# Output projection of a hybrid encoder layer: four row tiles summed in PSUM, two buffers for x, a new tile order

## The reference

```python
u = rms_norm(h, g_norm); z = u @ w_in
o_att = diff_attention(q, k, v, ...)          # per head: rms_norm(o, sub_norm) * (1 - lam_init)
o_lru = rg_lru_branch(xr, ...)                # two directions of a gated linear recurrence
mix = concatenate([o_att * silu(g_att), o_lru * silu(g_lru)], axis=-1)
h = h + mix @ w_out                           # the output projection
e = (p @ w_ple) * sigmoid(h @ w_pg)
h = h + rms_norm(e, g_ple)
```

## Time and profile before

| What | Value |
|---|---|
| median of 3 runs | 1044.59 us (1044.24 to 1045.69) |
| the profiled execution | 1044.89 us |
| its span | 1043.1 us |
| TensorE busy | 994.5 us (95%) |
| VectorE, ScalarE, GpSimd busy | 676.4, 641.4, 502.6 us |
| mean granted TensorE clock | 0.988 |
| DMA | 158.75 MB, 152 GB/s over the span |

### The profile page before, as it was taken

The page is one execution under the profiler, slowest core; times in us unless marked ns, Lnnn a source line. Parts: engine busy times, 40 slices in busy tenths (PEclk is TensorE's granted clock), DMA queues, the critical chain, the costliest instruction groups (busy, mean ns, idle before and its releaser), DMA issues.

```text
span 1043.1 us, 15702 instructions
## 1 busy us (share of the span) xinstructions
PE 994.5 (95%) x5720; PEld 787.3 (75%) x5720; DVE 676.4 (65%) x1115; ACT 641.4 (61%) x1058; POOL 502.6 (48%) x402
## 2 busy tenths in 40 slices
PE   8999999999999999989999999999979869999996
PEld 7867777777788888877777777777867657777775
DVE  5736766683672341699999999999536672444444
ACT  7747576655631222589999999999446542444442
POOL 1162435436665530265767667666422256554451
PEclk9999999999999999999999999999989889999999
DMA  9641544233347339489756764541857861122221
GB/s 345 266 137 36 172 147 118 100 101 124 111 139 219 104 100 262 129 213 256 202 155 168 179 168 134 139 143 62 282 154 226 279 219 51 45 87 91 74 76 74
DMA packets 108636, 158.75 MB, mean 152 GB/s; under 512 B 10504, under 2 KB 69384, under 8 KB 108552
## 3 DMA queue, kind: packets, MB, share of 16 engines
q1 hardware_dynamic: 108416, 157.75, 50.5%
q10 hardware_dynamic: 144, 0.00, 0.0%
HBM read 106.27 MB, written 48.30 MB: 148 GB/s over the span
## 4 chain that ended last, share of the span: by engine, by line
PE 65%; DVE 16%; issue 9%; DMA 4%; ACT 3%; POOL 1%; SPq 0%; DVEq 0%; POOLq 0%; ACTq 0%
DVE E_ L1895 9%; PE b_ps L2183 6%; PE b_ps L2321 6%; PE b_ps L2323 6%; PE b_ps L2322 6%; PE b_ps L2185 6%; PE b_ps L2184 6%; DMA x_rd<-in_x 3%; PE o_ps L2378 3%; PE s_ps L2334 3%; PE w_ps L2295 3%; PE uT_ps L2258 2%; DVE ratio L1904 2%; PE left_ps L2505 2%; PE left_ps L2508 2%
## 5 line engine op out<-in xcount | busy, mean ns | idle before, releaser
L1371 ACT ACTIVATE E_<-E_,nmax 128x1024 f32<-128x1024 f32 (+1 forms) x184 | 186.6, 1018 | 13.2 <-DVE nmax L1895 13.2
L1895 DVE CUSTOM_DVE_ANT_0 E_<-s_ps,bias 128x1024 f32<-128x1024 f32 (+1 forms) x184 | 188.2, 1056 | 10.0 <-PE s_ps L2334 9.8
L1070 POOL TENSOR_TENSOR E_<-E_,ratio 128x576 f32<-128x576 f32 (+3 forms) x92 | 84.7, 920 | 92.5 <-DVE E_ L1911 92.5
L1073 POOL TENSOR_TENSOR E_<-E_ 128x576 f32<-128x576 f32 (+3 forms) x92 | 103.7, 1127 | 7.2
L2185 PE MATMUL b_ps<-u_hi,wA_lo 128*128 128x512 f32 x256 | 99.8, 390 | 0.0
L2334 PE MATMUL s_ps<-KL,QL 128*128 128x512 f32 x256 | 88.6, 430 | 8.1 <-DVE nmax L1895 8.0
L1386 ACT ACTIVATE WT<-w_ps 128x1024 f32<-128x1024 f32 (+1 forms) x96 | 83.5, 870 | 5.9 <-PE w_ps L2295 5.3
L2183 PE MATMUL b_ps<-u_hi,wA_hi 128*128 128x512 f32 x216 | 85.5, 396 | 0.0
L2295 PE MATMUL w_ps<-ident,E_ 128*128 128x128 f32 x624 | 83.5, 273 | 2.1 <-ACT WT L1386 2.0
L2184 PE MATMUL b_ps<-u_lo,wA_hi 128*128 128x512 f32 x216 | 84.1, 389 | 0.0
L2378 PE MATMUL o_ps<-WT,V 128*64 128x128 f32 x1280 | 84.0, 278 | 0.0
(11 more groups left out here) (338 smaller groups left out, 2613.1 us busy)
## 6 DMA issues: line engine op xcount, KB each, us to landing
QL<-qk_t SPq DMA_DIRECT2D x32, 256.0 KB, 7.0
KL<-qk_t SPq DMA_DIRECT2D x32, 256.0 KB, 8.4
bias<-line_d SPq DMA_DIRECT2D x8, 960.0 KB, 11.7
x_sb<-in_x SPq DMA_DIRECT2D x12, 512.0 KB, 9.0
z_ch<-z_stage SPq DMA_DIRECT2D x24, 256.0 KB, 2.8
qk_t<-qh SPq DMA_DIRECT2D x24, 256.0 KB, 2.3
qk_t<-ql SPq DMA_DIRECT2D x24, 256.0 KB, 2.8
mf<-mix_t SPq DMA_DIRECT2D x24, 256.0 KB, 4.1
```

The source lines that it names most:

```text
L1073: gp.tensor_tensor(one, one, two, ALU.add).then_inc(w_gp, 1)
L1371: act.activation(e, e, ACT.Exp, bias=nmax[:, n % 5, c:c + 1], scale=-1.0, accum_out=sums[:, n % 5, c:c + 1]).then_inc(e_done, 1)
L1895: dve.tensor_tensor_reduce(weights_at(n)[:, c, 0:n_tok], s_ps[:, c, 0:n_tok], b[:, ::-1], -1.0, 3e38, ALU.add, ALU.min, nmax[:, n % 5, c:c ...
```

## The change

Four things are done together.

1. The tiles are visited in the order `SEQ = [0, 1, 8, 2, 9, 3, 10, 4, 11, 5, 6, 7]`. Everything in the loop now goes by position n, and the tile is `SEQ[n]`. Tiles 8 to 11 stand at the positions 2, 4, 6 and 8 (`WHOLE`); the others are `HALF`.
2. The half products of tiles 8 to 11 are no longer copied out, stored, reloaded and added. They stay in PSUM, and `mix_product` adds the attention's half to the same banks. For positions 4, 6 and 8 they are computed right ahead of their `mix_product`, behind T(n+1); those of tile 8 stay where they were and wait in banks 4 and 7 (`all_ps`).
3. x has two buffers, `x_rd[0]` and `x_rd[1]`, and its load waits for the position two back. At `WHOLE` positions VectorE adds x straight from `x_rd`.
4. What surrounds this is moved: `wp_raw` is loaded at position 8 instead of ahead of the loop, `gpB` after the loop instead of at position 3 (VectorE waits for it ahead of its first gate step), the square root's table is loaded by a dummy activation earlier, both GpSimd subtractions of gate weights go to VectorE, and `wp_lo` goes behind all `add_half`.

```diff
+        x_rd = [put("x_rd0", O_REGION + 16 * KB, [P, D]), put("x_rd1", MIX_IN + 8 * KB, [P, D])]
+        SEQ = [0, 1, 8, 2, 9, 3, 10, 4, 11, 5, 6, 7]
+        WHOLE = [SEQ.index(t) for t in range(8, NT)]
+        HALF = [i for i in range(NT) if i not in WHOLE]
...
-            return o_ps[:, 1, :] if j < IN_STEPS or j % 2 else right_ps[:]
+            return o_ps[:, 1, :] if j < IN_STEPS else mix_bank(SEQ.index(j // 2))[:, j % 2, :]
+        def mix_bank(i):
+            if i < 3:
+                return (h_ps[:], hq_ps[:], all_ps[:, 4:8:3, :])[i]
+            return h_ps[:] if i % 2 else hq_ps[:]
...
+            def load_x_again(n):
+                t = SEQ[n]
                 if n >= 2:
+                    if n - 2 in HALF:
+                        sp.wait_ge(fin["x_sum"], HALF.index(n - 2) + 1)
+                    else:
+                        sp.wait_ge(fin["h_done"], n - 1)
+                sp.dma_start(x_rd[n % 2][:], x[t * P:(t + 1) * P, :]).then_inc(fin[f"x_in{n % 2}"], 16)
...
+            store_o(1, HEADS // 2 - 1)
+            sp.wait_ge(o_st[1], 16 * 4)
             load_o(2)
+            load_mf(10)
...
+            sp.dma_start(gpB[:], bass.AP(tensor=g_ple.tensor, offset=0, ap=[[0, P], [1, D]])).then_inc(gain_in, 16)
...
             o_scale(1)
-            add_half(1)
+            for k in range(1, len(HALF)):
+                add_half(k)
             for k in range(PC):
                 gp.wait_ge(wp_hi_done, k + 1)
                 gp.tensor_tensor(wp_lo[:, k, :], wp_raw[:, k, :], wp_hi[:, k, :].bitcast(F32),
...
             mix_high(0)
             heads_out(2 * HEADS - 1)
-            half_out(IN_STEPS)
+            mix_high(1)
+            act.activation(mse[:, 0:1], neghalf[:, 0:1], ACT.Sqrt, scale=-2.0)
             square_o(2)
...
             def mix_product(n, between=None):
-                pe.wait_ge(fin["m_lo"], n + 1)
...
+                if n >= 3:
+                    pe.wait_ge(fin["h_done"], 1 if n == 3 else n - 1)
+                if n in WHOLE[1:]:
+                    half_tile(2 * SEQ[n])
+                    half_tile(2 * SEQ[n] + 1)
+                pe.wait_ge(fin["m_lo"], n + 1)
```

More of the change, by code:

```diff
@@ L272, in encoder_layer @@
         t4_lo = put("t4_lo", LRU_W + 24 * KB, [P, LC, 512], F32R)
[L274 to L276 removed]
+        wp_hi = put("wp_hi", LRU_W, [P, PC, D], F32R)
+        wp_raw = put("wp_raw", LRU_W + 8 * KB, [P, PC, D])
+        wp_lo = put("wp_lo", LRU_W + 8 * KB, [P, PC, D], F32R)
         o_in = [put(f"o_in{s}", O_REGION + 2 * KB * s, [P, A]) for s in range(2)]
@@ L862, in load_x_again, with load_hp @@
-            def load_x_again(n):
-                if n:
-                    sp.wait_ge(fin["x_sum"], n)
-                sp.dma_start(x_rd[:], x[n * P:(n + 1) * P, :]).then_inc(fin["x_in"], 16)
+            def load_hp(k):
+                t = SEQ[HALF[k]]
+                if k >= 2:
+                    sp.wait_ge(fin["h_done"], HALF[k - 2] + 1)
+                for b in range(2):
+                    sp.wait_ge(hp_out[b], 16 * t + 16)
+                sp.dma_start(hp_sb[:, k % 2, :], hpart[t * P:(t + 1) * P, :]).then_inc(fin[f"hp_in{k % 2}"], 16)
@@ L2175, in _, with product @@
             pe.wait_ge(ident_done, 3)
-            def product(dst, pairs, before=None):
+            def product(dst, pairs, before=None, start=True):
                 n = len(pairs)
@@ L2182, in product @@
                         before(k)
-                    pe.matmul(dst, sh, mh, start=k == 0, stop=False)
+                    pe.matmul(dst, sh, mh, start=start and k == 0, stop=False)
                     pe.matmul(dst, sh, ml, start=False, stop=False)
@@ L2408, in half_product @@
                 pe.matmul(dst, hi, wl_lo[:, k, c], start=False, stop=False)
-                mm = pe.matmul(dst, lo, wl_hi[:, k, c], start=False, stop=k == 3)
+                mm = pe.matmul(dst, lo, wl_hi[:, k, c], start=False, stop=k == 3 and j < IN_STEPS)
                 if k == 3:
@@ L2457, in mix_product @@
                     mm = product(mix_bank(n)[:, b, :], [(m_hi[n % 2][:, k, :], m_lo[n % 2][:, k, :], wa_hi[:, k, c],
-                                                         wa_lo[:, k, c]) for k in range(LC)])
+                                                         wa_lo[:, k, c]) for k in range(LC)], start=n in HALF)
                     if between and b == 0:
```

254 lines of the change are left out of this document (117 added, 137 removed).

## The result

| | before | after |
|---|---|---|
| median (range) | 1045.14 us (1044.24 to 1047.81, 4 runs) | 1027.77 us (1026.78 to 1031.78, 4 runs) |
| ratio, 95% interval | | 0.9837 [0.9805, 0.9869] |
| profiled execution, span | 1044.89, 1043.1 us | 1027.9, 1026.1 us |
| TensorE busy in the span | 994.5 us | 990.3 us |
| mean granted clock | 0.988 | 0.993 |

17.4 us are gone, 1.6%. The forecast was 1027.0 us. The steps behind it were not all right, though: a slow clock that I charged with 2.4 us behind T(2) was no cost, in the last twenty microseconds two errors cancel in part, and the ring that I had read in the profile of before turned out to be one of several.

What follows compares the result with a forecast made beforehand. It took the one-buffer x load and add, plus clock falls, to bound the kernel. A TensorE timetable moved the first gate product into `right_ps` from 876.07 to 858.2 us, 17.9 us off 1044.89: 1027.0 us, range 1023 to 1034.

Steps and rivals of the forecast that it cites:

- a slow clock: At the transpose and mix product following 5.0 us of TensorE idle time: 8.48 us instead of 6.09, a 2.4 us charge.
- the ring: Kernel before: load x, add, free its one buffer, load x; GpSimd waited 64.1 us, and SyncE's later loads waited too.
- Start of T(2): Transpose at position 2: after store, load of `o_in`, table load, square, root and `scale_o`, at 764.3 us.
- Rival 1: Store 7.4 us and load 5.7 us ahead of position 2's transpose, all later ones 5.5 us later: 1032.5 us, chance 0.17.
- my reading that traffic lengthened it: The 512 KB store's 7.4 us, against 2.3 us for a lone 256 KB one, put down to other transfers; about 4 us expected.
- The positions: Transposes at positions 3 to 11: ScalarE and VectorE's loop about 7 us, then TensorE the bound, 11.57 and 6.09 us by turns.
- rival 2: Transfers still set the pace in the loop, 9.1 us a position, first gate product into `right_ps` at 865.9: 1034.7 us, chance 0.08.
- From T(11) to p5: Last position's transpose to the first gate product into `right_ps`: GpSimd's load, adds and splits decide, 19.4 us against TensorE's 16.1.
- The wait ahead of p1 for `gpB`: Before the gate products: `gpB` issued about 842 us, landing 8.9 us, VectorE's first gate step at 851 us, p1 about 853.6.
- so no clock charge: Before the gate products: 3.3 us waiting splits into idle times near 1.5 and 1.8 us, both under 2.01 us, keeping the clock.
- Rival 4: SyncE's x load waits for `add_x`, blocking `load_o`; landing of 25 us gives 1053.6 us. Chance 0.03, plus 0.02 for gain eaten up.

Runs made afterwards that it cites:

- traffic: Changed kernel plus eight 512 KB DRAM-to-DRAM copies, one at each of positions 1 to 8: 1027.92 us, ratio 0.9836 to the kernel before.
- fill_gap: Changed kernel plus 20 overwritten matmuls in TensorE's idle time ahead of the transpose at position 2: 1028.39 us, ratio 0.9837 to the kernel before.
- early_wp: Changed kernel with `wp_hi` one position earlier and `wp_lo` ahead of GpSimd's last two adds of x: 1024.56 us, ratio 0.9801 to the kernel before.
- before_two_x: Kernel before with only a second x buffer, from tile 5 on: 1044.60 us, ratio 0.9999 to the kernel before.
- early_load_dve: Kernel before with two x buffers, three `o_in` buffers, earlier `o_in` loads and GpSimd's two gate-weight subtractions on VectorE: 1038.08 us, ratio 0.9927.
- together: Changed kernel with the four whole tiles at positions 2, 3, 4, 5 instead of 2, 4, 6, 8: 1032.61 us, ratio 0.9885 to the kernel before.

## Why the prediction was right, and where it was wrong

**Start of T(2).** Forecast 764.3 us, came at 764.97, but by another path. I had ScalarE as the last to be ready, from its table load, at 760.2 us, and `o_in` there at 759.5. ScalarE was free at 760.04 us and then waited 0.79 us for `o_in`, whose landing at 760.8 us set T(2). The store was issued at 752.72 us and landed 5.22 us later, the load of `o_in` 2.86 us after it; I had said 4 and 3 us. Rival 1 (7.4 and 5.7 us) did not come. From the chain of waits:

```profile
752.72 5.22 DMA o_tok<-O
757.96 2.86 DMA o_in<-o_tok
760.84 0.64 ACT O_sq L1467
```

The store lands 2.2 us sooner than the 7.4 us of before, which fits my reading that traffic lengthened it, though no run takes the traffic away alone. With x and the end of two loads of `mf` beside them, the 512 KB still took 5.2 us, more than my 4. The page "DMA: Bandwidth & Descriptors" of the Trainium skill, which I weighed against my reading, warns, of GpSimd's path, of the wait for the confirmation at the end of a write; this trace can't separate it from the bytes.

**The positions.** Forecast for T(3) to T(11): 772.8, 778.9, 785.8, 797.4, 803.5, 815.0, 821.1, 832.7, 838.8. Measured: 773.11, 779.15, 786.23, 797.83, 803.86, 815.37, 821.40, 832.91, 838.94. None is off by more than 0.45 us. From T(5) on this is the mechanism as forecast: TensorE is the bound. That the removed transfers are worth nothing by themselves in this order, and that rival 2 would not come, is shown by traffic as well. Between T(2) and T(5) the steps came as forecast too, with the slow clock first, but that the fall did no harm is luck: one slow position and one at full speed, 8.14 and 6.04 us, are together as long as two turns of the loop of 7.1 us. fill_gap shows it. With the clock kept all three positions take the loop's time, 786.44 - 765.19 = 21.25 us, against the 785.8 - 764.3 = 21.5 us of my sum. So the 2.4 us that I charged for the fall are in the sum, but the fall cost nothing.

**From T(11) to p5.** Forecast 19.4 us, measured 857.37 - 838.94 = 18.4 us. The chain was the one named: `add_x(9)`, load, add, `wp_lo`, `p_lo`, two `s_lo`. On GpSimd:

```profile
845.94 2.81 POOL L1117 TENSOR_TENSOR hp_sb<-hp_sb,x_rd 128x1024 f32<-128x1024 f32 x1 [1.62 <-DMA hp_sb<-hpart]
848.71 4.77 POOL L1127 TENSOR_TENSOR wp_lo<-wp_raw,wp_hi 128x1024 fp32r<-128x1024 f32 x2
853.43 1.43 POOL L1141 TENSOR_TENSOR p_lo<-p_sb,p_hi 128x256 fp32r<-128x256 f32 x2
854.83 3.75 POOL L1132 TENSOR_TENSOR s_lo<-s_raw,s_hi 128x512 fp32r<-128x512 f32 x3
```

The load landed in 4.33 us (in the chain of waits) instead of 5.4; the add took 2.81 us instead of 2.41. The wait ahead of p1 for `gpB` was wrong: it was issued at 841.87 us, the list of DMA issues has its landing at 5.2 us, and VectorE came to its first gate step only at 847.53 us. So there was one idle time of 2.16 us and not two of 1.5 and 1.8 us. VectorE's last subtraction, `t_lo`, which I had ending 5.7 us after its T, ended 7.5 us after it (the last section says why); behind GpSimd's chain it cost nothing.

**The step that failed** is "so no clock charge". The split into two idle times under 2.01 us didn't happen, and even had it, that bound came from a single row and doesn't hold (the last section). After 2.16 us the clock fell, with 0.55 granted in the row from 858 us on, and p5 took 861.81 - 857.37 = 4.44 us instead of 2.8 us:

```profile
858.00:860.00 2.00, 2.00 (x7) 1.57 (x6) 0.00 (x0) 0.00 (x0) 1.81 (x2) 0.55 0.00 0
```

p5 came 0.8 us earlier than forecast, the slow clock gave 1.7 us to what stands behind it, and the sum, 0.9 us under the span measured (1026.1 against 1043.1 - 17.9 = 1025.2 us), looks better than its parts. early_wp shows wait and clock by taking both away.

**What bounded the kernel before.** I called it the ring of x, and the runs show that this was one of four things that stand one behind the other: x, `o_in`, the order in SyncE's queue, and GpSimd beside VectorE. The profile of before already had a sign of it that I did not read, SyncE's own waits from 780 to 870 us:

```profile
SPq L852 <- DVE mr L1986: 30.2, 8, 6.9
SPq L865 <- POOL hp_sb L1099: 13.6, 5, 3.2
```

The load of x held the queue for 13.6 us, but that of `Gt`, which waits for `o_gate`, for 30.2 us. And GpSimd's wait for x, 64.1 us, does not go with the second buffer: in before_two_x it is 72.4 us, since x still comes only once a position. Freed one by one in the old order they gave: x alone 0 (before_two_x), `o_in` alone 2.7 us, both 2.5, with the load order 2.6 and with GpSimd's subtractions 6.0 us (each against the runs of before on its chip; steps of less than 2 us between them can't be told). In the new order, taking the second x buffer back costs 26 us. So the forecast stood on a right timetable of the kernel after, not on the right cause in the kernel before. Where I did price the removal of the ring, for before_two_x, I missed by 14 us.

**Rival 4** was priced from landings, at 3 in 100, and its mechanism was much nearer than I thought: one buffer fewer and SyncE's in-order queue carries the kernel past the one before. With the two buffers that the change has, the wait of the x load for `add_x` came to 3.0 us in all, and the ring did not close.

**What stays open.** The half products in PSUM were not undone by themselves: no run has the new order with the four tiles taken through DRAM. The 10.3 us between early_load_dve and the changed kernel are argued to be theirs, from together (4.8 us for their place alone) and from the idle time that they fill between T(5) and T(11), not shown; nor is it shown whether keeping them in PSUM matters beside doing them later, or what the moved `wp_raw` is worth ahead of T(2). Nor was an order of SyncE's list tried that would let one x buffer do without any loss.

## What to carry to other kernels

Where a load waits in an in-order queue, price what stands behind it and not the load: the same single buffer cost 26 us at one place in the list and 9 us one iteration later. A chain of waits names one ring; before betting on its removal, write the timetable of the engines with the ring gone, because a second of the same length may stand behind it, made of the same queue. And work that can be placed freely is worth most where it covers the loop that runs beside it, a little in every position, not in a heap.
